# Dilated heads: joining of statistics and what follows it, one block product later on DVE, ACT and TensorE

## What is computed

```python
def dilated_window_group(q, k, v, window, dil):      # for (128, 1), (512, 4), (2048, 16)
    ...
    s = jnp.where(valid[None, :, :, None], s + bias[None, None, None], NEG)
    m = jnp.max(s, axis=-1, keepdims=True)
    p = jnp.exp(s - m)
    l = jnp.sum(p, axis=-1, keepdims=True)
    o = jnp.einsum('bnrhij,bnjrhe->bnirhe', (p / l).astype(v.dtype), vn)
    lse = (m + jnp.log(l))[..., 0]
    ...

def dilated_mixer(qkv):
    ...
    wts = jax.nn.softmax(jnp.stack(lses, 0), axis=0)
    o = jnp.sum(wts[..., None] * jnp.stack(outs, 0).astype(F32), axis=0)
```

## Time and profile before

| | us |
|---|---|
| median of three runs | 2059.8 (2054.34 to 2060.3) |
| the profiled execution | 2058.21 |
| its span in the trace | 2056.5 |
| PE busy | 2011.7 (98%) |
| DVE, ACT, POOL busy | 1082.8, 804.3, 418.2 |
| mean granted clock of PE | 0.995 |

### The profile page before, as it was taken

How to read it: one execution, slowest core, us unless ns; L and a number is a source line. 1 busy time by engine, 2 the same in 40 slices (tenths; PEclk the granted TensorE clock), 3 DMA queues, 4 the chain that set the end, 5 groups by cost and what they waited for, 6 DMA issues and landing times. The chain is left out here.

```text
span 2056.5 us, 27177 instructions
## 1 busy us (share of the span) xinstructions
PE 2011.7 (98%) x9869; PEld 1639.6 (80%) x9869; DVE 1082.8 (53%) x1940; ACT 804.3 (39%) x1463; POOL 418.2 (20%) x343
## 2 busy tenths in 40 slices
PE   7999999999999999999999999999999999999998
PEld 4788888888888888888887787788888888767787
DVE  7644444454644655654645423587878783334312
ACT  5443323343433443433524412444444443223322
POOL 2341412323323323323300012301010100000011
PEclk9999999999999999999999999999999999999999
DMA  7332340433233233233243511311111111513422
GB/s 247 129 122 80 105 144 27 143 103 96 62 100 86 71 99 95 67 97 102 58 162 125 154 56 31 130 42 32 50 33 44 38 42 45 154 52 100 146 62 103
DMA packets 218343, 186.83 MB, mean 91 GB/s; under 512 B 9498, under 2 KB 191236, under 8 KB 217604
## 3 DMA queue, kind: packets, MB, share of 16 engines
q1 hardware_dynamic: 212960, 177.56, 28.7%
q0 software_dynamic: 4480, 6.66, 1.3%
q10 hardware_dynamic: 804, 1.33, 0.2%
HBM read 144.27 MB, written 41.25 MB: 90 GB/s over the span
## 5 line engine op out<-in xcount | busy, mean ns | idle before, releaser
L298 DVE TENSOR_TENSOR w_lo<-w_raw,w_hi 128x512 fp32r<-128x512 f32 x219 | 197.7, 904 | 166.1 <-ACT w_hi L294 165.8
L218 PE MATMUL z_ps<-b_parts,w_hi 128*128 128x512 f32 x680 | 274.7, 404 | 3.4 <-ACT g_gate L228 1.8
L220 PE MATMUL z_ps<-b_parts,w_lo 128*128 128x512 f32 x680 | 268.6, 395 | 0.0
L219 PE MATMUL z_ps<-b_parts,w_hi 128*128 128x512 f32 x680 | 268.4, 395 | 0.0
L321 PE MATMUL z_ps<-ah_hi,w_hi 128*128 128x512 f32 x512 | 210.0, 410 | 5.3 <-DVE qkv L913 3.1
L323 PE MATMUL z_ps<-ah_hi,w_lo 128*128 128x512 f32 x512 | 202.0, 395 | 0.0
L322 PE MATMUL z_ps<-ah_lo,w_hi 128*128 128x512 f32 x512 | 202.0, 395 | 0.0
L294 ACT ACTIVATE w_hi<-w_raw 128x512 fp32r<-128x512 f32 x224 | 138.3, 625 | 105.5 <-PE z_ps L323 54.0
L218 PEld LDWEIGHTS z_ps<-b_parts,w_hi 128*128 128x128 f32 x680 | 128.4, 189 | 36.6 <-issue 7.1
L220 PEld LDWEIGHTS z_ps<-b_parts,w_lo 128*128 128x128 f32 x680 | 128.2, 188 | 30.2
L219 PEld LDWEIGHTS z_ps<-b_parts,w_hi 128*128 128x128 f32 x680 | 128.5, 189 | 28.3 <-issue 0.5
(11 more groups left out here) (500 smaller groups left out, 4364.9 us busy)
## 6 DMA issues: line engine op xcount, KB each, us to landing
w_raw<-in_a_win SPq DMA_DIRECT2D x160, 256.0 KB, 3.3
w_raw<-in_b_win SPq DMA_DIRECT2D x33, 512.0 KB, 4.0
work<-in_a_win SPq DMA_DIRECT2D x48, 256.0 KB, 5.2
v_scratch<-qkv SPq DMA_DIRECT2D x12, 1024.0 KB, 5.2
work<-v_scratch SPq DMA_DIRECT2D x16, 512.0 KB, 5.6
y_scratch<-y SPq DMA_DIRECT2D x16, 512.0 KB, 3.4
w_raw<-in_a_wout SPq DMA_DIRECT2D x8, 768.0 KB, 5.6
w_raw<-in_b_wout SPq DMA_DIRECT2D x8, 768.0 KB, 5.9
```

Of the source, the lines that this page charges most:

```text
L218: pe.matmul(z_ps[s][:, 0:width], w_hi[slot][:, k, :], hi[k][:, tok], start=(k == 0), stop=False)
L219: pe.matmul(z_ps[s][:, 0:width], w_hi[slot][:, k, :], lo[k][:, tok], start=False, stop=False)
L220: mm = pe.matmul(z_ps[s][:, 0:width], w_lo[slot][:, k, :], hi[k][:, tok], start=False, stop=(k == nk - 1))
L298: eng.tensor_tensor(op_ring(w_lo, u), op_raw[i], op_ring(w_hi, u).bitcast(F32), ALU.subtract).then_inc(lo_op, 1)
```

## The change

On PE, ACT and DVE every piece from the join on moves from u to u + 1: the joins and `weights` to 28 and 32, `scale_natural` to 31 and 35, the turns to 30 to 37 (with the moves), `weighted_values` to 36 and 39, `finish` to 37 and 40. Scores, softmaxes and exponentials stay. Nothing is added or taken away. The lists of POOL (301 rows in the program) and SP (215 rows) are the same.

```diff
-                TURN = {29: 0, 30: 1, 31: 2, 32: 3, 33: 4, 34: 5, 35: 6, 36: 7}
+                TURN = {30: 0, 31: 1, 32: 2, 33: 3, 34: 4, 35: 5, 36: 6, 37: 7}
...
-                        if u == 35:
+                        if u == 36:
                             weighted_values(h, 1)
-                        if u == 38:
+                        if u == 39:
                             weighted_values(h, 0)
...
-                        if u in (27, 31):
-                            weights(h, 1 if u == 27 else 0)
+                        if u in (28, 32):
+                            weights(h, 1 if u == 28 else 0)
...
-                        if u in (27, 31):
-                            join(h, 1 if u == 27 else 0)
-                        if u in (30, 34):
-                            scale_natural(h, 1 if u == 30 else 0)
-                        if u in (36, 39):
-                            finish(h, 1 if u == 36 else 0)
+                        if u in (28, 32):
+                            join(h, 1 if u == 28 else 0)
+                        if u in (31, 35):
+                            scale_natural(h, 1 if u == 31 else 0)
+                        if u in (37, 40):
+                            finish(h, 1 if u == 37 else 0)
```

## The result

| | before, us | changed, us |
|---|---|---|
| median of the timed runs | 2056.7 (2054.34 to 2060.3, 5 runs) | 2080.4 (2075.78 to 2083.44, 5 runs) |
| ratio to before | | 1.0106 [1.0087, 1.0124] |
| the profiled execution | 2058.21 | 2083.44 |
| its span | 2056.5 | 2081.8 |
| waits of TensorE in the heads | 3.9 | 23.6 |

The change makes the kernel 1.1% slower, and the median is the one forecast. The sum behind it is not: about 3/5 of the difference are later joins, and most of the rest goes with TensorE's loop over the heads, which was not in the forecast. I take the trace in the order in which the prediction did.

What follows compares the result with a forecast made beforehand. TensorE, busy 98% of the span, was taken to bound the kernel, with at most 3.9 us to gain. 2.14 + 0.34 = 2.48 us in each of eight heads, 19.8, added to 2059.8 gave 2080 us, range 2069 to 2092.

Steps and rivals of the forecast that it cites:

- What bounds the kernel: TensorE, busy 98% of the span; at most 3.9 us of waits removable; joining work must end by product 13.
- First join: Join of s = 1 on DVE, u 27 to 28: 3.66 us later, by itself costing nothing.
- The four issues, each 3.66 later: POOL's factors out and in, statistics out and in, each 3.66 us later; statistics land at 709.74.
- Second join = the later of landing and low part of 15: Join of s = 0 on DVE starts at 709.85, set by operation 15's low part over the landing's 709.74: 3.77 us later.
- Join to product 13: From the second join through scalings (4.34), addition (0.67) and hand-over (0.13): product 13 at 714.99, net 2.14 us late.
- The mis-sized term: Heads that already waited pay about the same again, so 2.48 us for each of eight heads, 19.8 us.
- My lower bound: Least landing times in every head: 0.7 us less per head, +14 us; with the factors' transfers fast too, +11.
- the rival: Clock falls after TensorE's idling in the heads: 13.6 us more, 2094, or 2084 for two or three; most heads 0.12.
- my own signs of being wrong: L1194 of s = 0 at its old place, clock falling in the heads, or another line than L913 holding product 13.
- Landing in time: Later second join finds its data; about 0.1 us a head, 2061 us; within 0.3% had chance 0.05.
- not slower: Statistics of s = 0 not behind the factors in POOL's queue; waits go, 2056; faster by over 0.3% had 0.01.
- Half: Later sums miss the scalings, or landings are fast: 1.0 to 1.6 us a head, 2068 to 2072; chance 0.12.

Runs made afterwards that it cites:

- the single edit: Kernel before with only the first join (s = 1) and its ACT step moved, u 27 to 28: 2071.3 us, 1.0058.
- written-out pair: Kernel before and changed kernel, each with TensorE's loop over heads 2 to 7 written out, no branch back: 2053.3 and 2065.4 us.
- the run with the sums between: Changed kernel with POOL making sums L273 and L277 between the store of the statistics of s = 0 and their load: 2063.3 us, 1.0024.
- the last comparison: Kernel before and changed kernel, with the loop (2055.2 and 2076.1 us) and with it written out (2053.3 and 2065.4 us).
- the statistics out first: Changed kernel with POOL sending the statistics of s = 0 out ahead of the factors of s = 1: 2066.9 us, 1.0044.
- later turns: Kernel before with only TensorE's turns and value products, ACT's moves and DVE's finishes behind them, one product later: 2057.8 us, 1.0002.
- the same edit: Statistics of s = 0 sent out ahead of the factors of s = 1 on POOL: changed kernel 2066.9 us, kernel before 2074.5 us.

## Why the prediction was right, and where its working was not

*What bounds the kernel.* Right: busy time stayed, idle time grew; the deadline is product 13 and the waits are ended by L913 and L1358, once or twice in each head.

*First join.* 3.66 us later, at no cost by itself: measured 3.7 in the mean. That its cost comes by POOL's queue was right, and the single edit shows it (13.0 us for this part, nothing for the second sequence's joins).

*The four issues, each 3.66 later.* The store is 3.1 us later in the mean, the load 3.2.

*Second join = the later of landing and low part of 15.* Right in kind: it is the low part. The low part took 1.18 us for the 0.90 taken from the page, so the join comes 1.88 us after the end of L273 (715.46 to 717.34) where the sum had 1.62. The landing is no rival any more: 2.0 us at the median and 2.7 at most, where the earlier trace rows had 2.5 and 5.1, and in every head it is through before the low part is.

*Join to product 13.* 4.98 us (717.34 to 722.32), 5.14 forecast.

*The mis-sized term* is the last: "The heads that waited already pay about the same again, since their late landing moves too". The forecast took one head's 2.48 us times eight, 19.8. Measured are 15.1 us more waits in the profiled pair, 1.9 a head, and 11.3 with the loop written out, 1.4 a head. What didn't persist are the late landings: in before the second join hung on the load's landing, in two heads at 39.4 us of the head and later; now it hangs on L273, and a load that takes long costs nothing there. A head that was late before therefore had less to lose. The profiled pair shows it head by head: the three heads that did not wait in before wait 2.4 to 3.1 us now, as forecast, and the five that did wait pay 1.3 us more in the mean. In the written-out pair the two kinds of head pay 1.4 us alike; there the load itself goes out only 2.6 us later (34.9 to 37.5), where the forecast moved it by 3.66. In the means the join moved by 3.6 us in the profiled pair (38.4 to 42.0), product 13 by 1.5 (45.4 to 46.9) where 2.14 stood, and the join by 3.2 in the other (38.1 to 41.3), and not by 3.77.

My lower bound (+11 to +14) came near this, at the least landing times, but its working has a misreading: the landing times of the earlier trace rows count from the start of an issue (in the run with the sums between, a join follows a load by 2.01 us from its start and 1.44 from its end, and the least landing time there is 1.8), and I added them to its end, 701.86 and not 701.10. Put right, the load would go out 0.76 us earlier and the lower bound is lower by as much in each head, near +8.

*What was missing:* TensorE's loop, 8.8 us of the 20.9, of which the idle time at the branches is about half (4.4 us in the changed kernel's trace). That the rest comes from the branches too is not shown. I had weighed a fall of the clock (the rival) in the heads' own waits, which never came in those; it came behind the second branch, in both traces of the changed kernel (6.8 and 3.4 us of lower clock), so one of my own signs of being wrong did show in one head. The two errors are of like size and opposite sign (in the last comparison 19.8 for 12.1, and nothing for 8.8), which is why 2080 was met. The base helped as well: the forecast was added to 2059.8, the median of three runs, and with two more it is 2056.7, so in the first comparison the difference was 23.7 us and not 19.8. The number is luck; the path by the joins is not. Without the loop's part the change costs 12 us, in the lowest part of my range.

*The rivals.* "Landing in time" and "not slower" fell: the store took 4.0 us to land at the median, its later issue is real, and the statistics do stand behind the factors. "Half" (1.0 to 1.6 us a head) is what the joins alone cost in the written-out pair. The "not slower" mechanism exists nevertheless: with the statistics out first the changed kernel's join waits are 4.7 us, near before's 3.9.

*Still open:* why TensorE's loop stays loaded in some executions and not in others. TensorE's order of before had none or one long branch in each of four traces, later turns had one in one trace and two in five; with more instructions ahead of the loop it was two with either order. Order alone does not decide it, and position alone neither, since one execution has both kinds of branch with the same code in the same place. Not run is the changed kernel with the statistics out first, or the sums between, and the loop written out; from 2066.9 and 2063.3 with 4.3 and 6.5 us at the branches it could come near 2055, by my estimate, which would be level with before and no gain. The only version that ran faster than before is before with its loop written out, by 1.9 us, less than what can be told from no change.

## What to carry to other kernels

Follow an edit through every in-order queue that it feeds, and ask for each transfer behind it what it truly depends on. Here a join that nobody waited for was delayed; its factors stood in GpSimd's queue ahead of statistics that had nothing to do with it, and ahead of a weight sum, and those were what TensorE waited for. A row names only the last release: the one just before it decides what moving the first is worth, as the same edit showed by gaining 12 to 15 us in one kernel and losing 18.5 in the other.

When a sum over a few heads meets the total, look whether each of its terms met its own row. And compare the branch and instruction-queue rows of two traces: the branch back of a long loop can cost several us, in some executions only.

## What the runs showed of the hardware that I had not expected

TensorE's branch back took 0.21 to 0.25 us in one turn and 5.1 to 8.1 us in another of the same code, with nine more packets of 16 KB on the instruction queue. The wait that it makes is shown as "issue" or under whoever released something last (L298), not as a branch.

A matmul of one column is not small. In the kernel with 70 of them, which the trace has as 140, they take 25 us (first row), and the profile shows, by stretch (PE and PEld busy, then DVE, ACT, POOL; the clock third from the end):

```profile
437.64 24.96 PE L1271 MATMUL s_ps<-qkv 128*128 128x1 f32 x140
...
443.00:466.90 23.90, 23.90 (x105) 23.03 (x105) 1.65 (x8) 1.09 (x4) 0.00 (x0) 0.50 0.02 7
```

TensorE was busy throughout, by its records, and was granted the lower clock for 23.9 us, from 5.4 us after the first of these matmuls on; the weight loads fill 23.03 of them. At the higher clock 47 of the matmuls took those 5.4 us, at the lower one 93 took 19.4: 0.11 and 0.21 us each.
